# Expert rows added into two sums per token by the scattering DMA, in a one-core hybrid SSD / attention / MoE block

## What is computed

```python
n2 = rms_norm(h, norm2_g[i]) * (1.0 + sc2) + sh2
ff = moe_ffn(n2, ...)                 # 64 experts, hidden 256, top 6 of 64 per token, one shared expert
h = h + g2 * ff
return rms_norm(h, final_g)

# moe_ffn
scores = sigmoid(n @ router_w);  top 4 of 8 groups, then top 6 experts by scores + bias
w = w / sum(w) * 2.5
out = (silu(n @ s_gate) * (n @ s_up)) @ s_down
for e in range(64):
    hid = silu(n @ e_gate[e]) * (n @ e_up[e])
    out = out + (hid @ e_down[e]) * combine[:, e:e + 1]
```

## Time and profile before

| | |
|---|---|
| median of 3 runs | 1402.02 us (1400.27 to 1402.16) |
| the profiled execution's own time | 1402.26 us |
| its span, first to last instruction | 1400.6 us |
| mixer / opening of `moe` / expert units / end | 0 to 671 / 671 to 767 / 767 to 1346.9 / 1346.9 to 1400.6 us |
| PE busy, PE weight load busy | 88%, 46% |
| DVE, ACT, POOL busy | 31%, 19%, 14% |
| bytes moved by DMA | 318 MB, mean 227 GB/s |

### The profile page before, as it was taken

The page is one execution under the profiler, slowest core; times in us unless marked ns, Lnnn a source line. Parts: engine busy times, 40 slices in busy tenths (PEclk is TensorE's granted clock), DMA queues, the critical chain, the costliest instruction groups (busy, mean ns, idle before and its releaser), DMA issues. The chain is left out here.

```text
span 1400.6 us, 13583 instructions
## 1 busy us (share of the span) xinstructions
PE 1238.9 (88%) x4905; PEld 642.3 (46%) x4905; DVE 440.3 (31%) x934; ACT 264.4 (19%) x639; POOL 193.0 (14%) x313
## 2 busy tenths in 40 slices
PE   3999999887999999999767799998899989978856
PEld 1536865565554454468433344443334434433322
DVE  4575024545566101112263122221212212211116
ACT  2141121123441000000201122221212212211101
POOL 4000011111002000000125121111111121221101
PEclk9999999998999998999879799999999999998988
DMA  9531211103448231210752689999999999999655
GB/s 300 154 120 60 90 60 56 35 31 121 120 139 283 90 120 42 78 60 0 303 231 79 211 333 350 420 420 419 416 411 408 400 395 409 396 396 416 269 229 211
DMA packets 106778, 318.07 MB, mean 227 GB/s; under 512 B 14212, under 2 KB 67544, under 8 KB 80728
## 3 DMA queue, kind: packets, MB, share of 16 engines
q1 hardware_dynamic: 87152, 269.37, 50.2%
q0 software_dynamic: 18080, 43.07, 8.7%
q10 hardware_dynamic: 1480, 4.77, 0.9%
HBM read 310.29 MB, written 26.79 MB: 241 GB/s over the span
## 5 line engine op out<-in xcount | busy, mean ns | idle before, releaser
L1670 PE MATMUL ps<-gu_w,xsT 128*64 128x512 f32 (+1 forms) x1024 | 316.7, 634 | 46.9 <-issue 26.7
L1670 PEld LDWEIGHTS ps<-gu_w,xsT 128*64 128x64 f32 (+1 forms) x1024 | 119.0, 163 | 215.1 <-issue 214.5
L1678 PE MATMUL ps<-dn_w,hidT 128*64 128x512 f32 (+1 forms) x512 | 152.4, 597 | 1.0 <-ACT hidT L1340 1.0
L1518 DVE SCALAR_TENSOR_TENSOR hid<-ps,wgt,gated 128x256 f32<-128x256 f32 x42 | 20.3, 484 | 342.7 <-ACT gated L1344 342.7
L927 PE MATMUL ps<-n1T,ring 128*128 128x512 f32 x256 | 113.0, 603 | 3.7 <-DVE keep_mod L675 3.0
L707 PE MATMUL ps<-n1T,ring 128*128 128x512 f32 x256 | 111.9, 594 | 0.0
L1248 POOL DMA_INDIRECT expert_rows<-hn,meta x42 | 42.9, 1021 | 424.1 <-DVE hn L1514 403.3
L1678 PEld LDWEIGHTS ps<-dn_w,hidT 128*64 128x64 f32 (+1 forms) x512 | 52.4, 153 | 69.9 <-issue 67.4
L927 PEld LDWEIGHTS ps<-n1T,ring 128*128 128x128 f32 x256 | 49.4, 194 | 65.6 <-issue 61.7
L1344 ACT ACTIVATE gated<-ps 128x256 f32<-128x256 f32 x42 | 16.1, 383 | 333.8 <-PE ps L1670 333.8
L707 PEld LDWEIGHTS ps<-n1T,ring 128*128 128x128 f32 x256 | 48.2, 190 | 58.7 <-issue 58.7
(11 more groups left out here) (311 smaller groups left out, 1222.3 us busy)
## 6 DMA issues: line engine op xcount, KB each, us to landing
gu_w<-in_exp_w_gate_dram SPq DMA_DIRECT2D x64, 1024.0 KB, 16.8
gu_w<-in_exp_w_up_dram SPq DMA_DIRECT2D x64, 1024.0 KB, 28.4
dn_w<-in_exp_w_down_dram SPq DMA_DIRECT2D x64, 1024.0 KB, 23.2
ring<-in_w_in_dram SPq DMA_DIRECT2D x24, 1024.0 KB, 5.6
keep_h<-in_ada_w_dram POOLq DMA_DIRECT2D x32, 512.0 KB, 4.9
gu_w<-expert_rows SPq DMA_DIRECT2D x4, 2048.0 KB, 17.1
ring<-in_w_branch_ssd_dram SPq DMA_DIRECT2D x4, 1024.0 KB, 5.5
ring<-in_w_branch_attn_dram SPq DMA_DIRECT2D x4, 1024.0 KB, 6.0
```

The costliest lines, as they stand in the source:

```text
L1670: ins = pe.matmul(ps[rows, 2 + b, :], xsT[:, b, k, rows], gu_w[:, s, :, k, :], start=(k == 0), stop=(k == KC - 1))
L1678: ins = pe.matmul(ps[rows, 5 + half, :], hidT[:, jj, rows], dn_w[:, s, jj, BANK * half:BANK * half + BANK], start=(jj == 0), stop=(jj == 1))
```

## The change

Each row is now added to a sum in DRAM by the DMA itself, in place of being stored apart. There are two sums per token, `expert_sums[0:512]` for rows that a unit holds in partitions 0 to 63 and `expert_sums[512:1024]` for those in 64 to 127; list words 2 and 3 carry the two row numbers (token, and 512 + token). The parts:

- ACT issues, ahead of its other stores, one DMA that writes zeros over the 4 MB of `expert_sums` from a zeroed `gated` (2 KB pieces); POOL clears `gated` first, and ACT waits for the DMA (`zeroed`) before it writes `gated` for the shared expert.
- POOL fills one more word of the empty list and of the entries (two more iotas, one more memset).
- The scatter has `compute_op=ALU.add`, and waits for the scatter before it (`scattered[1 - b]`) as well.
- At the end SP loads two rows per token, four DMAs of 1 MB; PE's 64 instructions of identity matmuls and DVE's L1568 are gone.

```diff
-    rows_d = nc.dram_tensor("expert_rows", [NROW, D], F32, kind="Internal").ap()
+    rows_d = nc.dram_tensor("expert_sums", [2 * SEQ, D], F32, kind="Internal").ap()
...
-            rows_v = rows_d.rearrange("(t p k) d -> p t (k d)", p=P, k=TOPK)
-            for t in range(T):
-                sp.dma_start(gu_w[:, t, :, :, :].rearrange("p a k f -> p (a k f)"), rows_v[:, t, 0:4 * D]).then_inc(rows_in[t], 16)
-                sp.dma_start(flat(dn_w[:, t, :, :]), rows_v[:, t, 4 * D:]).then_inc(rows_in[t], 16)
+            rows_v = rows_d.rearrange("(c t p) d -> t p c d", c=2, p=P)
+            for t in range(T):
+                sp.dma_start(dn_w[:, t, :, :], rows_v[t]).then_inc(rows_in[t], 16)
...
+            pool.memset(gated[:, :, :], 0.0).then_inc(const_step, 1)
...
-            for w in (0, 2):
+            for w in (0, 2, 3):
...
-            pool.iota(pay[:, :, :, 2], [[P * TOPK, T], [1, TOPK]], base=0, channel_multiplier=TOPK,
-                      allow_small_or_imprecise_dtypes=True).then_inc(const, 1)
+            for copy in range(2):
+                pool.iota(pay[:, :, :, 2 + copy], [[P, T], [0, TOPK]], base=SEQ * copy, channel_multiplier=1,
+                          allow_small_or_imprecise_dtypes=True).then_inc(const, 1)
...
-            def scatter(c, b, done):
+            def scatter(c, b, done, others):
+
+                pool.wait_ge(zeroed, 16)
                 pool.wait_ge(ordered, ORDER)
+                if not isinstance(others, int) or others > 0:
+                    pool.wait_ge(scattered[1 - b], others)
                 pool.wait_ge(y_act, done)
                 pool.wait_ge(y_dve, done)
                 pool.indirect_dma_start(
                     out=rows_d[:, :], out_offset=bass.IndirectOffsetOnAxis(ap=meta[:, c, 1:2], axis=0),
-                    in_=ys[:, b, :], in_offset=None, bounds_check=last_row, oob_is_err=False).then_inc(scattered[b], 16)
+                    in_=ys[:, b, :], in_offset=None, bounds_check=last_row, oob_is_err=False,
+                    compute_op=ALU.add).then_inc(scattered[b], 16)
...
-            act.wait_ge(const, 5)
+            act.wait_ge(const_step, 5)
+            act.dma_start(rows_d.rearrange("(p r) (s c) -> p (r s) c", p=P, c=2 * FF),
+                          flat(gated[:, :, :]).unsqueeze(1).broadcast_to([P, 2 * 2 * SEQ // P, 2 * FF])).then_inc(zeroed, 16)
+            act.wait_ge(const, 6)
...
+            act.wait_ge(zeroed, 16)
             shared_gate(0)
...
-                dve.tensor_copy(meta[HALF:P, c, :], entry(1, col)[:, 0:3:2]).then_inc(upper_done, 1)
+                dve.tensor_copy(meta[HALF:P, c, :], entry(1, col)[:, 0:4:3]).then_inc(upper_done, 1)
...
                 total = dn_w[:, t, 0, :]
-                dve.wait_ge(rows_in[t], 32)
+                dve.wait_ge(rows_in[t], 16)
                 chain(dve.tensor_tensor(total, total, dn_w[:, t, 1, :], ALU.add))
-                dve.wait_ge(tail_sum, t + 1)
-                chain(dve.tensor_tensor(total, total, flat(ps[:, 2 * t:2 * t + 2, :]), ALU.add))
                 chain(dve.tensor_tensor(total, total, g2_row[:, :], ALU.mult))
...
-            for t in range(T):
-                pe.wait_ge(rows_in[t], 32)
-                rows = gu_w[:, t, :, :, :].rearrange("p a k f -> p (a k f)")
-                for half in range(2):
-                    for k in range(4):
-                        ins = pe.matmul(ps[:, 2 * t + half, :], ident[:, :],
-                                        rows[:, D * k + BANK * half:D * k + BANK * half + BANK], start=(k == 0), stop=(k == 3))
-                ins.then_inc(tail_sum, 1)
```

More of the change, by code:

```diff
@@ L1096, in moe @@
         rows_in = [sem(f"rows_in{t}") for t in range(T)]
-        tail_sum, fsq_in, fin_done, stored = sem("tail_sum"), sem("fsq_in"), sem("fin_done"), sem("stored")
+        fsq_in, fin_done, stored, zeroed = sem("fsq_in"), sem("fin_done"), sem("stored"), sem("zeroed")
         block = ctx.enter_context(nc.Block())
@@ L1180, in _ @@
                       allow_small_or_imprecise_dtypes=True).then_inc(const, 1)
-            pool.wait_ge(const_step, 4)
+            pool.wait_ge(const_step, 5)
             pool.affine_select(out=low[:, :, :], in_=low[:, :, :], compare_op=ALU.is_gt, fill=0.0,
@@ L1223, in _ @@
             pool.wait_ge(lists_in, 32)
-            last_token, last_row = pool.to_reg(SEQ - 1), pool.to_reg(NROW - 1)
+            last_token, last_row = pool.to_reg(SEQ - 1), pool.to_reg(2 * SEQ - 1)
             def lower(u):
@@ L1265, in _ @@
                 if u >= 1:
-                    scatter((u - 1) % 6, (u - 1) % 2, u)
+                    scatter((u - 1) % 6, (u - 1) % 2, u, 16 * (u // 2))
             count = load_turns(pool)
@@ L1271, in _ @@
                     ready, filled = done + 1, done * 2 + 6
+                    others = j * (16 * LAST // 2) + 16 * ((BEFORE + m) // 2)
                     col = from_table(j, m + 2)
-                    pool.to_reg(done), pool.to_reg(ready), pool.to_reg(filled), pool.to_reg(col)
+                    pool.to_reg(done), pool.to_reg(ready), pool.to_reg(filled), pool.to_reg(col), pool.to_reg(others)
                     pool.wait_ge(lists_rest, 32)
@@ L1276, in _ @@
                     gather((m + 2) % 6, m % 2, col, filled)
-                    scatter((m - 1) % 6, (m - 1) % 2, done)
+                    scatter((m - 1) % 6, (m - 1) % 2, done, others)
             units, each = count * LAST + BEFORE, count * (16 * LAST // 2) + (16 * BEFORE // 2 + 16)
-            pool.to_reg(units), pool.to_reg(each)
-            scatter(5, 1, units)
+            others = count * (16 * LAST // 2) + 16 * BEFORE // 2
+            pool.to_reg(units), pool.to_reg(each), pool.to_reg(others)
+            scatter(5, 1, units, others)
             for b in range(2):
@@ L1404, in _ @@
             own = gs[:, :, :].unsqueeze(3).broadcast_to([P, T, RGROUPS, RGROUPS])
-            dve.wait_ge(const, 7)
+            dve.wait_ge(const, 9)
             dve.tensor_tensor(cmp[:, :, :, :], other, own, ALU.is_gt)
@@ L1459, in _ @@
             shared_hid(0)
-            dve.wait_ge(const, 14 + FIXED)
+            dve.wait_ge(const, 16 + FIXED)
             chain(dve.scalar_tensor_tensor(out=keys, in0=ps[0:HALF, 5, 0:NE], scalar=float(NE), in1=tie[:, :],
```

## The result

The changed kernel takes 1437.73 us (1436.85 to 1438.67, 4 runs) against 1402.09 us before (1400.27 to 1402.61): a ratio of 1.0257, 95% interval 1.0239 to 1.0274. It is slower by 35.6 us, where 8.4 were forecast. The profiled execution took 1438.67 us with a span of 1437.0.

What follows compares the result with a forecast made beforehand. The prediction took the expert units to be bound by DMA engine time, with PE close behind. From 1402.26 us, end -19.6, last scatter +1.0, adds +27.0 and zeros 0 gave 1410.7 us, own range 1407 to 1420, 8-in-10 range 1382 to 1440.

Steps and rivals of the forecast that it cites:

- the end: From the last scatter's landing to DVE's last addition to h: fewer loads and no PE sums, -19.6 us (-20.1 to -15.2).
- the first landing: At the end, the first of four 1 MB loads lands 5.5 us after the last scatter, between bounds 5.0 and 10.0.
- DVE's pitch: At the end, DVE's time per group without L1568, 5.03 us, with DVE the late one.
- The last scatter: Before the final loads: it must read the sums before writing them, +1.0 us (0 to +2.6).
- Its new wait for the scatter ahead I cost at nothing: At the last scatter: the scatter ahead lands in 2 to 5 us, behind the last unit's down product and copies; 0.
- I take the added read at the price of a move: In the expert units: the add's second read costs DMA engine time like a plain move, full passage +28.5 us.
- Cost 0, with +4 as the high end: At the opening: 4.19 MB of zeros land before the first gate and the list DMA need them; 0 to +4 us.
- the pessimistic end: At the opening: zeros come last but for 2.6 MB of other stores and land at 721 us, instead of 708.
- I take +27: In the expert units from 850 us: the adding scatters' extra DMA time, 25.5 to 28.5 us, up to 3 absorbed by rest.
- The second read is free: Rival for the units: the add costs no engine time and the end's gain stays, 1383.7 us; chance 0.22.
- half hidden: Rival for the units: an added row costs half a move more, +14 us, 1397.7 us; chance 0.10.
- The serial scatters set the pace: Rival for the units: scatter landings of 15.4 us, past the deciding 13.7, set each unit's time, +62, 1445.6 us; chance 0.18.

Runs made afterwards that it cites:

- e3: As e1, but scatters of odd units add to a tensor of their own, so no scatter waits for the one ahead; 1416.64 us, ratio 1.0128.
- e5: The kernel before, with each unit's rows stored a second time by a plain scatter to another tensor; 1443.08 us against 1406.91, ratio 1.0249.
- e1: The changed kernel with the 4 MB of zeros stored in the mixer and not at the opening of moe; 1417.64 us, ratio 1.0141 against the kernel before.
- e4: The kernel before with only the zeroing DMA of the change and its wait before the first gate; 1421.48 us, ratio 1.0162.
- e2: As e1, but the scatter stores in place of adding, the waits between scatters kept; 1380.12 us, ratio 0.9857 against the kernel before.
- e7: As e4 with half of the zeros (2 MB, 1024 pieces of 2 KB); 1407.93 us against 1406.91 for the kernel before, ratio 1.0004.
- e8: The kernel before, with PE at the end waiting for its four rows only and DVE for the two others; 1405.07 us against 1406.91, ratio 0.9982.
- e9: As e8, plus ten unused PE matmuls ahead of the final sums; 1404.23 us against 1406.83 for the kernel before, ratio 0.9981.
- e6: The changed kernel with the zeros issued after ACT's two other stores and its modulation of n2T; 1429.28 us, ratio 1.0170 against the kernel before.

## Why the prediction was wrong

**Right: the end.** -19.6 us was forecast and -20.1 measured; the first landing (5.1 against 5.5 us), DVE's pitch (5.02 against 5.03) and its being the bound came out by their rows. The last scatter: +1.0 forecast; it lands in 1.9 us more and starts 0.6 later. "Its new wait for the scatter ahead I cost at nothing" was right for the units (e3) and 0.6 us short here.

**Right: what the add is.** "I take the added read at the price of a move" stood on the earlier trace rows, loads and stores sharing one budget. e5 and e1 confirm it: 36.2 and 37.5 us by the medians, 41.2 and 40.5 by the traces of the units, for the same 12.6 MB.

**Wrong: "Cost 0, with +4 as the high end" for the zeros.** The measured term is 20.7 us (21.9 in e4), and it is the larger part of the miss. The step counted when the zeros and the stores behind them would have landed, and who needs them. The landing itself came out late but harmless: 708 was computed and 721 the pessimistic end, it was 723.4, and the first gate, delayed by then anyhow, waited 0.8 us for it. What the step left out is the time of an issue, which it took for free. Behind ACT's next issue stood the modulation of n2T, which had nothing to do with the zeros. The sign of it was in the trace of before and I passed over it: SP's issues of the fixed experts' loads take mostly 0.3 to 0.7 us each at first and, with some ten in flight, 2.4 to 4.9 us each. In the timeline of SP before:

```profile
677.92 0.68 SPq L1120 DMA_DIRECT2D gu_w<-in_exp_w_gate_dram  x1
678.64 4.87 SPq L1121 DMA_DIRECT2D gu_w<-in_exp_w_up_dram  x1
683.56 3.34 SPq L1124 DMA_DIRECT2D dn_w<-in_exp_w_down_dram  x1
```

SP has nothing else to do and its stand costs nothing; ACT computes. The prediction had named the sign by which it would be wrong here, POOL's first list copy over 1 us later than 765.45: it came at 786.15.

**Wrong in size: "I take +27" for the adds.** The units' stretch grew by 39.1 us, with 28.0 forecast. The last scatter's 2.5 us aside, 36.6 us of it are the adds. By e1 and e2 the add's own engine time was 29.9 where a full passage was put at 28.5, the weights took 1.4 more, and the engines' moments of rest, which were to swallow up to 3 us, grew by 5.7. The forecast let the rest absorb work; it did the opposite, and it did so in e5 without any add. What makes it grow with the load was not tried alone. The rows it goes with are PE's: longer holes, a granted clock down from 0.96 to 0.93 over the stretch (e2 and e1), and slots that come free later. On the page, gate and up take more time for the same 1024 instructions, 316.7 us before:

```profile
L1680 PE MATMUL ps<-gu_w,xsT 128*64 128x512 f32 (+1 forms) x1024 | 329.6, 663 | 70.4 <-issue 49.3
```

**The rivals.** "The second read is free" and "half hidden" fall by e5 and e2. "The serial scatters set the pace" falls by e3: landings went from 8.5 to 10.2 us in the median (12.3 at most), under the 13.7 from which it was to decide. The time lay near that rival's region (1440.7 to 1445.6) all the same, for another reason, so its nearness bears out nothing of the rival.

**Not forecast: the last stretch**, 3.3 us shorter. From DVE's last instruction to the end it is 7.7 us in the kernel before, e2, e4, e7, e8 and e9, and 4.4 in the changed kernel, e1, e3, e5 and e6, counted from that instruction's start. The difference lies behind the work: the last store lands 3.8 us before the span's end in the kernel before and 0.5 us before it in the changed kernel. e2 and e1 have the same end, so it isn't the end's code; why it has two lengths stays open. It hides 3.3 us of the adds' cost: between e2 and e1 the medians differ by 37.5 us, and the units by 40.5.

**The sum of the miss**, by the two traces: 36.4 us measured against 8.4 forecast. Of these 28.0 us the opening has 20.7, the adds 9.6, the last scatter 1.5, the end -0.5 and the last stretch -3.3.

Two readings of the prediction are off, without effect on the sum: slices 25 to 37 of the strip are 840 to 1296 us, not 860 to 1310, and with its own terms POOL's share would be 85.5 us of 502, 17.0% and not 18 (measured: 17.6%).

## What to carry to other kernels

An accumulating DMA moves its row once by the byte count and twice by the engines' time, so in a stage with full DMA engines "add on the way" pays only if it saves more bytes than its reads, the clearing and the final loads cost; here 12.6 + 4.2 + 4.2 MB took the place of 12.6 MB of final reads. A DMA of many pieces can hold the engine that issues the next one, so put it last, or on a queue whose engine has nothing to do, and look for long issue times in the old trace before costing it at nothing. DMA work moved into a stage whose DMA engines are full is paid for in full, here with some 10 us on top of the 30 that the engines spend on it, even where the profile shows every other engine with idle time.

## What the runs showed of the hardware that was not expected

- ACT's queue takes 64 pieces of 2 KB per DMA engine, and the next store, without holding the issuing engine (issue of the next store 0.43 us); with 128 pieces that issue took 24 us (e7, e4).
- The issue of an adding scatter keeps POOL 1.57 us in place of 1.02.
- An adding scatter with no weights in flight lands in 4.5 us in place of 2.6, and under the weights in 10.2 in place of 8.5 in the median (e1, e2): 1.7 to 1.9 us more either way.
- A second read from DRAM by the adding DMA costs the kernel as much as a second store of the same bytes (40.5 and 41.2 us in the units, e1 and e5).
- 1.92 us of idle time after 8.8 us of dense matmuls went with a granted clock of 0.85 in the ten microseconds that followed (e9).
